# Exact causal key ranges, and the last output row interleaved with the first feed-forward tiles

## The reference

```python
# first layer (h = rmsnorm(x)); dq, dk, dv: 4 heads of "difference" attention; fq, fk, fv: 8 "forget gate" heads
p  = softmax(where(chunk_mask, q1 k1, NEG)) - lam * softmax(where(chunk_mask, q2 k2, NEG));  od = p @ dv
pf = softmax(where(causal, fq fk * scale + cum_q - cum_k, NEG));                             of = pf @ fv
x = x + concat(rmsnorm(od), of) @ w_out
x = x + (silu(h2 @ w_gate) * (h2 @ w_up)) @ w_down          # h2 = rmsnorm(x), 2816 hidden columns
x = rmsnorm(x)
# second layer: two causal convolutions (3 and 31 taps) and 8 "stick-breaking" heads
a  = where(s < t, exp(log_beta + suffix), 0);  y_c = a @ v
x = x + concat(y_a, y_b, y_c) @ w_out_2
x = x + square(relu(h2 @ w_ff1)) @ w_ff2                    # 4096 hidden columns
out = rmsnorm(x)
```

## Time and profile before

| | us |
|---|---|
| median of three runs | 2684.67 |
| the profiled execution | 2683.63 |
| its span | 2681.8 |
| PE busy | 2554.7 |
| VectorE busy | 1264.0 |
| ScalarE busy | 930.6 |
| GpSimd busy | 866.1 |

### The profile page before, as it was taken

The page is one execution under the profiler, slowest core; times in us unless marked ns, Lnnn a source line. Parts: engine busy times, 40 slices in busy tenths (PEclk is TensorE's granted clock), DMA queues, the critical chain, the costliest instruction groups (busy, mean ns, idle before and its releaser), DMA issues.

```text
span 2681.8 us, 31274 instructions
## 1 busy us (share of the span) xinstructions
PE 2554.7 (95%) x11998; PEld 2081.6 (78%) x11998; DVE 1264.0 (47%) x1862; ACT 930.6 (35%) x1541; POOL 866.1 (32%) x613
## 2 busy tenths in 40 slices
PE   7988999999899999999999988999999999999996
PEld 5666778878688888888887866787778888888884
DVE  6677778784543112212335997777341121121213
ACT  4455555552422112212234116555242131221321
POOL 6755541211522222222233343331342222222232
PEclk9999999999899999999999989999999999999997
DMA  3311321231111111111112222122111111111111
GB/s 136 83 40 48 91 60 32 59 108 62 41 52 51 48 48 48 47 52 51 47 49 85 80 67 59 52 70 92 60 49 50 52 48 48 48 48 51 51 48 67
DMA packets 85971, 159.25 MB, mean 59 GB/s; under 512 B 10560, under 2 KB 17088, under 8 KB 85696
## 3 DMA queue, kind: packets, MB, share of 16 engines
q1 hardware_dynamic: 85824, 157.26, 19.0%
HBM read 123.14 MB, written 15.20 MB: 52 GB/s over the span
## 4 chain that ended last, share of the span: by engine, by line
PE 79%; DVE 14%; issue 3%; ACT 2%; POOL 1%; DMA 0%; SPq 0%; POOLq 0%; DVEq 0%; ACTq 0%
PE PS L1169 23%; PE PS L1171 23%; PE PS L1170 23%; DVE CV L1582 3%; PE PS L1238 2%; DVE sm L1387 2%; PE PS L1254 2%; PE PS L1257 1%; PE PS L1223 1%; PE PS L1229 1%; DVE R L1495 1%; DVE Pb L1410 1%; DVE Pb L1408 1%; POOL mix L1812 1%; DVE X L1478 1%
## 5 line engine op out<-in xcount | busy, mean ns | idle before, releaser
L1169 PE MATMUL PS<-R,wh 128*128 128x512 f32 x3088 | 1227.8, 398 | 42.1 <-POOL wl L1806 21.0
L1171 PE MATMUL PS<-R,wl 128*128 128x512 f32 x3088 | 1209.7, 392 | 0.0
L1170 PE MATMUL PS<-R,wh 128*128 128x512 f32 x3088 | 1209.6, 392 | 0.0
L1806 POOL TENSOR_TENSOR wl<-raw,wh 128x512 fp32r<-128x512 f32 (+2 forms) x406 | 543.2, 1340 | 1500.1 <-ACT wh L1635 1499.5
L1169 PEld LDWEIGHTS PS<-R,wh 128*128 128x128 f32 x3088 | 584.7, 189 | 167.6 <-issue 25.6
L1171 PEld LDWEIGHTS PS<-R,wl 128*128 128x128 f32 x3088 | 583.5, 189 | 123.9
L1170 PEld LDWEIGHTS PS<-R,wh 128*128 128x128 f32 x3088 | 584.8, 189 | 116.0 <-issue 3.8
L1635 ACT ACTIVATE wh<-raw 128x512 fp32r<-128x512 f32 (+2 forms) x406 | 246.6, 610 | 917.8 <-PE PS L1171 915.9
L1482 DVE TENSOR_TENSOR X<-PS,X 128x512 f32<-128x512 f32 x112 | 77.4, 691 | 459.5 <-PE PS L1171 459.5
L1706 ACT ACTIVATE PT<-PS 128x512 fp32r<-128x512 f32 x200 | 117.1, 596 | 97.8 <-PE PS L1238 90.7
L1238 PE MATMUL PS<-ident,Pb 128*128 128x128 f32 x800 | 116.8, 275 | 13.5 <-DVE Pb L1408 6.5
(11 more groups left out here) (212 smaller groups left out, 2179.6 us busy)
## 6 DMA issues: line engine op xcount, KB each, us to landing
raw<-w_ff_dram SPq DMA_DIRECT2D x128, 256.0 KB, 2.7
raw<-w_in_dram SPq DMA_DIRECT2D x92, 256.0 KB, 2.6
R<-R SPq DMA_DIRECT2D x96, 128.0 KB, 2.3
raw<-w_gate_dram SPq DMA_DIRECT2D x44, 256.0 KB, 2.7
raw<-w_up_dram SPq DMA_DIRECT2D x44, 256.0 KB, 2.6
raw<-w_down_dram SPq DMA_DIRECT2D x32, 256.0 KB, 2.6
X<-xT_dram SPq DMA_DIRECT2D x8, 512.0 KB, 8.2
scr_mix<-mix SPq DMA_DIRECT2D x8, 512.0 KB, 2.6
```

The costliest lines, as they stand in the source:

```text
L1169: e.matmul(PS[:, b, :], T.wh[:, h, kc], high, start=(k == 0), stop=False)
L1170: e.matmul(PS[:, b, :], T.wh[:, h, kc], low, start=False, stop=False)
L1171: m = e.matmul(PS[:, b, :], T.wl[:, h, kc], high, start=False, stop=(k == nk - 1))
L1806: e.tensor_tensor(T.wl[:, n % 4, 0:m], T.raw[:, n % 3, 0:m], T.wh[:, n % 4, 0:m].bitcast(F), ALU.subtract).then_inc(*sg.up("w_lo", n))
```

## The change

Five edits.

1. Key ranges are exact: n = 128*(i+1). Maximum, exponential, division, sigmoid and scan run over n keys. Scores run over n or, where that leaves less than 256 columns for a product, 256. The mask has 128 columns. The last key tile of a group is transposed for the later query tile only, and its products with V have 128 columns.
2. The last output row is interleaved with the first two feed-forward tiles. Row e of the second pass goes to banks 0 to 3, the two tiles (gate 0 and up 0; in the second layer w_ff1 tiles 0 and 1) hold banks 4 to 7 and take channel tile k as soon as it is normalised, from two rows behind.
3. The weights of row 7 come as two pieces of four output tiles each instead of eight pieces of one, a load of 4 x 128 columns.
4. The last projection marks each channel tile that it has read, so `row_split` waits for its own row only.
5. The taps' `later` is 180 instead of 100.

```diff
-            self.pieces.append((name, e, k, min(4, k0 + nk - k)))
+            self.pieces.append((name, e, k, min(4, k0 + nk - k), False))
+    def plan_across(self, name, e, k):
+        self.pieces.append((name, e, k, 4, True))
...
+    def dense_across(self, name, e, src, evac, ready, s):
+        piece = self.pieces.index((name, e - e % 4, s, 4, True))
...
+        for half in range(2):
+            b, given = self.next_bank()
+            self.step("mm", t=t, half=half, k=0, nk=1, b=b, given=given, src=src, s=s, kc=e % 4, piece=piece, ready=list(ready[s]),
+                      mark=False, frees=half == 1 and e % 4 == 3)
...
-        n = 256 * (i // 2 + 1)
+        n = 128 * (i + 1)
...
-        freed = [O.last_dense]
+        freed = [[("dense", ("read", O.last_read, k))] for k in range(8)]
...
-                split_row(0, got, src, ready, freed, att)
+                split_row(0, got, src, ready, freed[0], att)
...
+    def start_ffn(second, tiles, src, ready, dim, eps, acc):
+        gen = O.dense_together(tiles, src, ready, banks=[4, 5, 6, 7])
+        for e in range(8):
+            next(second)
+            if e == 0:
+                O.dense_banks = [0, 1, 2, 3]
+            if e > 1:
+                next(gen)
+        next(gen)
+        O.rstd_ready = O.rsqrt("mix", dim, eps, "rstd", [acc] + O.rstd_ready, banks=[0, 1])
+        run(second)
+        run(gen)
+        O.dense_banks = list(range(8))
...
-                   later=100)
+                   later=180)
...
+def spans(n):
+    if n <= 256:
+        return [(0, 256)]
+    if n <= 512:
+        return [(0, n)]
+    return [(0, 512), (512, max(n, 768))]
...
-                if k1 == n:
-                    e.matmul(S2[:, n - 256:n], T.identb[:, :], T.maskb[:, i % 2, :], start=False, stop=False)
+                if k1 >= n:
+                    e.matmul(S2[:, n - 128:n], T.identb[:, :], T.maskb[:, :], start=False, stop=False)
...
+                    if kt == 2 * s["c"] + 1:
+                        if par == 0:
+                            continue
+                        at = 256
...
-            k0, k1 = slice(0, 256), slice(256, 512)
+            k0, k1 = slice(0, 256), slice(256, 384) if kp == c else slice(256, 512)
+            o0, o1 = PS[:, ob, 0:256], PS[:, ob, 128:256] if kp == c else PS[:, ob, 0:256]
...
-            e.activation(T.PT[:, s["x"], 0, :], PS[:, s["tb"], :], ACT.Copy, bias=bias).then_inc(*sg.up("pt_hi", key))
+            m = 384 if s["kp"] == s["c"] else 512
+            e.activation(T.PT[:, s["x"], 0, 0:m], PS[:, s["tb"], 0:m], ACT.Copy, bias=bias).then_inc(*sg.up("pt_hi", key))
```

More of the change, by code:

```diff
@@ L303, in plan_ffn @@
                 for w in up:
-                    self.plan_tile(w, i, 0, 8)
+                    if (w, i) not in before:
+                        self.plan_tile(w, i, 0, 8)
             for e in range(8):
@@ L394, in rsqrt, with project @@
         return done
-    def project(self, u, name, tiles, src, prev, freed, ready=None, together=None):
+    def project(self, u, name, tiles, src, prev, freed, ready=None, together=None, last=False):
         later, evacs = [], []
@@ L460, in project @@
                 continue
-            for _ in self.dense(name, tiles[which], 0, 8, src, evac, ready if which == 0 else None):
+            if last and which == 2:
+                self.last_read = self.n + 1
+            for _ in self.dense(name, tiles[which], 0, 8, src, evac, ready if which == 0 else None,
+                                mark=last and which == 2):
                 yield
@@ L543, in group_steps @@
             self.turned += 1
-            O.step("turn", u=u, g=g, kp=kp, slot=slot, p=[("p", j["key"]) for j in jobs], tb=tb, given=given, x=x, pt=list(self.pt_given[x]))
+            O.step("turn", u=u, g=g, kp=kp, c=c, slot=slot, p=[("p", j["key"]) for j in jobs], tb=tb, given=given, x=x, pt=list(self.pt_given[x]))
             if kp == c:
@@ L962, in evac_u @@
             hr[i] += [("hid_hi", ("f1", key)), ("hid_lo", ("f1", key))]
-        gen = O.dense("w_gate", t, 0, 8, src, evac_g, src_ready)
         if t == 0:
-            for _ in range(6):
-                next(gen)
-            make_rstd(S, EPS1, ("acc2", ("n2", 7)))
-        run(gen)
-        run(O.dense("w_up", t, 0, 8, src, evac_u))
+            start_ffn(second, [("w_gate", 0, evac_g), ("w_up", 0, evac_u)], src, h_ready, S, EPS1, ("acc2", ("n2", 7)))
+        else:
+            run(O.dense("w_gate", t, 0, 8, src, evac_g))
+            run(O.dense("w_up", t, 0, 8, src, evac_u))
     ready2 = [[] for _ in range(8)]
@@ L1171, in tensor_program @@
             m = e.matmul(PS[:, b, :], T.wl[:, h, kc], high, start=False, stop=(k == nk - 1))
-            if k == nk - 1:
-                m.then_inc(*sg.up("dense", *([(t, half), ("piece", s["piece"])] if half else [(t, half)])))
-            elif half == 1 and k % 4 == 3:
-                m.then_inc(*sg.up("dense", ("piece", s["piece"])))
+            done = [(t, half)] if k == nk - 1 else []
+            if s["frees"]:
+                done.append(("piece", s["piece"]))
+            if s["mark"]:
+                done.append(("read", t, k))
+            if done:
+                m.then_inc(*sg.up("dense", *done))
         elif kind == "lambda":
```

157 lines of the change are left out of this document (88 added, 69 removed).

## The result

The changed kernel took 2639.71 us (median of 4 runs, 2635.15 to 2642.14) beside 2685.25 for the kernel before (2683.21 to 2686.18): ratio 0.9829, 95% interval 0.9812 to 0.9846. Compared once more later it took 2638.09 us, ratio 0.9824 (0.9811 to 0.9838). That is 45 to 48 us; the forecast was 2636 us, a gain of 48. In the profiled executions the span went from 2681.8 to 2640.4 us, 41.4; the profiled execution after was the slowest of its four.

A forecast was written before the change was run, and what follows sets the result against it. TensorE (PE), busy 95% of the span, was taken as the bound. Terms 19 + 21 + 3 + 5 = 48 us off 2683.6 gave 2635.6, median 2636; own range 2622 to 2650, 8-in-10 range 2619 to 2659.

The forecast's parts named there:

- the two starts: Start of either feed-forward: interleaved output rows and larger weight pieces cut 50.8 us to 41.4, gain 9.4 twice, 19 us.
- exact key ranges: Both attentions: PE sheds 19.5 us of work and 2 us of waiting goes, 21 us.
- rows freed singly: Start of the mixed heads: only rows 0 and 1 move ahead, 1.5 us each time, 3 us.
- taps: Convolution and second attention: of PE's 19.5 us of waits, 5 us go as the attention starts earlier.
- the first loss: Each feed-forward start: PE's first gate product waits 1.3 us for row 0 of the normalised input.
- The 3.5 us of further waits: Each feed-forward start: late VectorE subtractions, passed on whole from row to row, make PE wait 3.5 us in all.
- the 2.0 us for a bank held until rstd: Each feed-forward start, after the sum over partitions: PE meets a bank still held for 2.0 us.
- The 2 us for a shorter softmax: Attention stretches: VectorE's work shrinks 5%, so 5% of PE's 45 us of waiting goes, 2 us.
- (1): Attentions: V's products of 128 columns run at float32's rate; time 2658 us, chance 0.18.
- (2): Second attention's first unit: the taps hold c1 back and PE's filler is missing; price 5 + 12, 2653 us, chance 0.12.
- (3): Feed-forward starts become VectorE's and the clock falls again; gain 3 each for 9.4, 2649 us, chance 0.15.
- (4): Attentions: PE sheds work, softmax does not shorten, granted clock falls to 1.2 GHz; slower, 2690 us, chance 0.04.

## Why the prediction was right, step by step

| step | forecast | measured |
|---|---|---|
| the two starts | 19 | 24.5 by the distances, 26.7 alone |
| exact key ranges | 21 | 14.2 alone, 17 by its distances |
| rows freed singly | 3 | 2.9 in place, 0 to 3 |
| taps | 5 | 1.8, with about 3 either way |
| sum | 48 | 45 to 48 |

The sum was right, in part by luck: the starts gave 5 us more than their term and the key ranges 4 to 7 less, and these cancelled.

**The starts, too small.** The mechanism was as forecast: the small pieces' wait went, the half clock went (0.87 to 1.00), PE stayed the bound from row to row, the sum over partitions cost 1.7 us for 1.9, and the first loss was 1.6 and 2.0 for 1.3. The 144 products of each start took 36.0 and 36.4 us, less even than the 38 to 45 that were to show the mechanism. Two terms in it were too large. The 3.5 us of further waits: a late subtraction was to be passed on whole from row to row. It was not, since each subtraction has two rows of PE's work in front of it; VectorE stood idle 1.28 us before three of the eight, in rows of 4.1, and only the last row, which has least work in front of it, cost 1.7. And the 2.0 us for a bank held until rstd, which came as 1.0 and 0: I worked it out for one start from the 12.8 us of the earlier trace rows and took it for both, and rstd came to its first reader 11.6 and 9.6 us after the sum began. Together 4.8 + 1.9 + 2.0 = 8.7 lost for 6.1 and 5.5, that is 2.6 us more gained in the first start and 3.2 in the second. What the kernel with the pieces only shows was not in my reasoning: I added up the pieces' wait and the rows' wait as if each could go by itself, but behind the one stands the other.

**The key ranges, too large.** PE's own share is 8.7 (transposes) + 6.0 (scores) + 1.6 (V) + 0 (mask) = 16.3 us where I had 19.5. The transposes and V were right: 0.109 and 0.009 saved a product for 0.109 and 0.011 forecast. The step that failed is the mask: I took 0.015 us between 0 and 0.053, and it was 0. The row for 0 was there: the mask's own start to the next was 0.04 us and the rest fell on the product behind it, which hinted that its columns were not what cost. The Trainium skill, "TensorE: Matmul & The Clock Gate", section "LDWEIGHTS (loading the stationary operand)", gives a weight load as its columns over 1.2 GHz, 107 ns for 128. The estimate worked out from that figure was that a product under 256 columns costs its load. The trace agrees: V saved 0.009 us, the mask 0.000, a removed transpose 0.109. By that estimate PE's share would have been 3 us smaller, and right. The 2 us for a shorter softmax were not found either: the kernel with the long one loses 0.1 us by it, though 2 us lie within the noise of that comparison. The widths of the scores, 6.0 us of work, cost only 0 to 4 when put back; whether they are hidden in waits or given back by the clock stays open.

**Rows and taps.** The rows brought 2.9 us in their place, for 3 forecast, but in the first layer alone, where the forecast had 1.5 in each. The taps' 5 us were not found: the medians differ by 0.0 and 1.7 us, and 5 is at the edge of the 1.8 +- 3 of the means. The forecast priced the waits that go, and with 180 PE is idle 8.3 us less than with 100; it had no term for the half-clock spells that now fall on products (5.2 us more busy time).

**The rivals.** (1), float32 rate of V's narrow products, is out: 0.455 us for four. (2), c1 held back: in the second attention PE waited 2.7 us for a low part of K or V (one wait, after), nowhere near 12. (3), starts bound by VectorE and GpSimd: slow subtractions were there (up to 3.50 us), but they made one wait of 1.4 us a start, and the clock did not fall. (4), the clock in the attentions: it is small. The key ranges alone ran at a mean clock of 0.979 for 0.981 before; by 1.5 us for 0.001 that is about 4 us given back. The changed kernel as a whole has a higher clock, 0.986, since the starts' spells are gone.

## What to carry to other kernels

Where a dependent stage begins row by row, issue it interleaved with the rows that feed it, some rows behind, with banks of its own: on top of the larger pieces that was worth four times what removing the longest visible wait alone gave (9.8 for 2.5 us), since behind each wait stood the next one. Before narrowing a product look at what its start-to-start distance follows; where it does not follow the columns (0.000 us for the mask, 0.009 for V's 128-column products) narrowing saves next to nothing. Removing whole instructions from the bound engine paid some four fifths of their price; shortening the work of engines beside it paid nothing that four runs could show.

## What was not expected of the hardware

- A bf16 product of 128 or 256 columns with other weights than its neighbours costs 0.12 us either way: 0.04 to the next start and 0.08 more on the product behind it (0.20 us from the start of a 256-column product to the next, for 0.12 elsewhere). The 192 masks are 23 us of PE.
- The same program had half-clock spells in the first attention in one execution (mean clock 0.93 over 60 to 160 us) and hardly any in another (0.98), with PE busy 91.3 and 91.1 us of 100.
- The first 192 dense products of the same program took 63 us in one execution and 66 in another.
